# Mixed keys of the HGRN2 layer in two buffers: VectorE writes the updated half into the next level's buffer, GpSimd brings only the resting half

## What is computed

```python
def step(state, inp):                      # per head, forward; the backward pass flips time
    qc, kc, vc, gc = inp
    b = jnp.cumsum(gc, axis=2)             # gc = log f, f the forget gate
    diff = b[:, :, :, None, :] - b[:, :, None, :, :]
    decay = jnp.exp(jnp.where(causal, diff, -jnp.inf))
    attn = jnp.einsum('bhid,bhjd,bhijd->bhij', qc, kc, decay)
...
o_f = _gla_chunks(qh, k_f, vh, lf_f)
o_b = flip(_gla_chunks(flip(qh), flip(k_b), flip(vh), flip(lf_b)))
```

## Time and profile of the kernel before

| | us |
|---|---|
| median of 3 runs | 1420.4 (1419.1 to 1421.58) |
| the profiled execution's own time | 1419.64 |
| its span, first to last instruction | 1417.8 |
| TensorE matmul busy | 1355.3 (96%) |
| VectorE busy | 511.1 (36%) |
| GpSimd busy | 176.6 (12%) |
| heads of the HGRN2 layer | about 690 to 1026 of the span |

### The profile page before, as it was taken

How to read it: one execution, slowest core, us unless ns; L and a number is a source line. 1 busy time by engine, 2 the same in 40 slices (tenths; PEclk the granted TensorE clock), 3 DMA queues, 4 the chain that set the end, 5 groups by cost and what they waited for, 6 DMA issues and landing times.

```text
span 1417.8 us, 16281 instructions
## 1 busy us (share of the span) xinstructions
PE 1355.3 (96%) x6751; PEld 611.1 (43%) x6751; DVE 511.1 (36%) x908; ACT 193.9 (14%) x327; POOL 176.6 (12%) x118
## 2 busy tenths in 40 slices
PE   8999999989999999799999999999799999999995
PEld 4444464633333333344555555555446333333322
DVE  1244863432111111520455556555545221111107
ACT  1025400100000000111111111111011000000000
POOL 0000400050000001100222233222200400000020
PEclk9999989999999999999999999999999999999998
DMA  9920155468999994543222102200094789999952
GB/s 348 356 73 1 73 224 207 175 241 311 416 406 426 409 426 181 214 119 131 60 60 60 40 21 59 59 0 0 1 384 190 276 330 421 410 423 409 388 206 91
DMA packets 82888, 305.75 MB, mean 216 GB/s; under 512 B 5444, under 2 KB 49800, under 8 KB 70408
## 3 DMA queue, kind: packets, MB, share of 16 engines
q1 hardware_dynamic: 61728, 262.81, 47.7%
q10 hardware_dynamic: 16488, 25.21, 4.9%
q0 software_dynamic: 4608, 16.78, 3.1%
HBM read 271.23 MB, written 33.55 MB: 215 GB/s over the span
## 4 chain that ended last, share of the span: by engine, by line
PE 67%; issue 21%; DVE 6%; POOL 3%; ACT 1%; ACTq 1%; DVEq 0%; POOLq 0%
PE ps L559 24%; PE ps L594 11%; PE ps L460 8%; PE ps L517 7%; PE ps L702 4%; POOL W L1586 2%; PE ps L715 2%; PE ps L544 2%; PE ps L509 1%; PE ps L582 1%; PE ps L613 1%; PE ps L485 1%; PE ps L498 1%; PE ps L651 1%; PE ps L524 1%
## 5 line engine op out<-in xcount | busy, mean ns | idle before, releaser
L559 PE MATMUL ps<-W,S 128*32 128x512 f32 (+1 forms) x2048 | 336.7, 597 | 2.3 <-DVE S L1397 2.3
L715 PE MATMUL ps<-hT,W 128*128 128x512 f32 x512 | 232.5, 593 | 0.7 <-ACT W L845 0.7
L559 PE MATMUL ps<-S 128*64 128x512 f32 (+1 forms) x512 | 223.1, 593 | 0.5 <-DVE S L1397 0.5
L594 PE MATMUL ps<-W,hT 128*32 128x512 f32 (+1 forms) x1024 | 171.4, 594 | 1.7 <-DVE hT L1411 1.0
L559 PEld LDWEIGHTS ps<-W,S 128*32 128x32 f32 (+1 forms) x2048 | 97.9, 114 | 148.0 <-issue 143.7
L715 PEld LDWEIGHTS ps<-hT,W 128*128 128x128 f32 x512 | 92.8, 191 | 90.3 <-issue 88.5
L594 PE MATMUL ps<-S,hT 128*32 128x512 f32 (+1 forms) x256 | 113.2, 594 | 1.0 <-issue 1.0
L1586 POOL TENSOR_TENSOR W<-S,sq 128x512 f32<-128x512 f32 x56 | 83.8, 1497 | 145.3 <-DVE S L1494 110.6
L845 ACT ACTIVATE hT<-ps 128x512 f32<-128x512 f32 x82 | 46.5, 599 | 387.4 <-PE ps L594 287.0
L559 PEld LDWEIGHTS ps<-S 128*64 128x64 f32 (+1 forms) x512 | 61.8, 123 | 71.9 <-issue 70.5
L460 PE MATMUL ps<-W,hT 128*128 128x512 f32 x192 | 83.0, 593 | 0.7 <-ACT hT L845 0.7
(11 more groups left out here) (231 smaller groups left out, 1332.3 us busy)
## 6 DMA issues: line engine op xcount, KB each, us to landing
W<-moe_w_gate SPq DMA_DIRECT2D x24, 2048.0 KB, 12.5
W<-moe_w_up SPq DMA_DIRECT2D x24, 2048.0 KB, 13.2
W<-moe_w_down SPq DMA_DIRECT2D x24, 2048.0 KB, 11.4
S<-moe_w_gate SPq DMA_DIRECT2D x8, 2048.0 KB, 13.6
S<-moe_w_up SPq DMA_DIRECT2D x8, 2048.0 KB, 13.4
S<-moe_w_down SPq DMA_DIRECT2D x8, 2048.0 KB, 16.7
W<-w_in_odd SPq DMA_DIRECT2D x32, 512.0 KB, 6.3
slot_rows<-S ACTq DMA_DIRECT2D x4, 2816.0 KB, 19.4
```

The source lines that it names most:

```text
L559: last = pe.matmul(ps[a:a + n, bank, :], xgT[:, c, a:a + n], w[L][slot_of(e)][:, c, :], start=(c == 0), stop=(c == ND - 1))
L594: last = pe.matmul(ps[a:a + n, 2 + half, :], hidT[:, c, a:a + n], wd[L][slot_of(e)][:, c, half * 512:(half + 1) * 512], start=(c == 0), st ...
L715: last = pe.matmul(ps[:, f % 2, :], ring[slot][:, f, c, :], hT[:, c, :], start=(c == 0), stop=(c == ND - 1))
```

## The change

`K2` keeps its meaning for the keys that rest at a level. The mixed keys now live in `km[u % 2]`. VectorE multiplies those that stay mixed at the next level (the outer quarters of each 4s block) straight into `km[(u + 1) % 2]`, and writes the other updated ones (the inner quarters) to `K2`; both are instructions of 256 elements, and both are issued ahead of VectorE's wait for level u's own matmuls. GpSimd brings the 256 resting keys of the next level from `K2` into the other quarters of the buffer, one level earlier than its whole copy came, and runs eight such copies a head. The long-range products read `km`. `prepare` writes the mixed keys of level 1 and the rest by two strided tensor_scalar of 512 elements in place of one of 1024, and `ksum` adds the two under alternating rows.

```diff
@@ -239,7 +239,7 @@
         off_ps, off_done = sem("off_in_psum"), sem("off_done")
         hpv_ps, hout_done, hsq_done, sq_added = (sem(n) for n in (
             "hpv_in_psum", "hout_done", "hsq_done", "sq_added"))
-        keys_updated, keys_mixed = sem("keys_updated"), sem("keys_mixed")
+        keys_updated, keys_joined = sem("keys_updated"), sem("keys_joined")
         ssq_ps, rms_var, rms_std, rms_done = sem("ssq_in_psum"), sem("rms_var"), sem("rms_std"), sem("rms_done")
         stored = sem("out_stored")
         dve_order, pool_order = sem("dve_order"), sem("pool_order")
@@ -723,9 +723,8 @@
                     pe.wait_ge(prepped, hd + 1)
                 if level == 2:
                     pe.wait_ge(diag_done, hd + 1)
-                if level >= 1:
-                    pe.wait_ge(keys_mixed, hd * LEVELS + level)
                 if level >= 2:
+                    pe.wait_ge(keys_joined, hd * 8 + level - 1)
                     pe.wait_ge(updated, hd * 8 + level - 1)
                 if level >= 3:
                     pe.wait_ge(level_done, hd * LEVELS + level - 2)
@@ -740,19 +739,21 @@
 
             def gram_off(hd):
 
+                pe.wait_ge(keys_joined, hd * 8 + 7)
                 pe.wait_ge(updated, hd * 8 + 7)
                 for j in range(NT):
                     i = j ^ 1
-                    last = pe.matmul(ps[:, 4, j * P:(j + 1) * P], K2[:, j % 2, j * P:(j + 1) * P],
+                    last = pe.matmul(ps[:, 4, j * P:(j + 1) * P], km[0][:, j * P:(j + 1) * P],
                                      Q2[:, i % 2, i * P:(i + 1) * P], start=True, stop=True)
                 last.then_inc(off_ps, 1)
 
             def gram_pairs(hd):
+                pe.wait_ge(keys_joined, hd * 8 + 8)
                 pe.wait_ge(updated, hd * 8 + 8)
                 for j in range(NT):
                     i = 1 - j // 2
                     last = pe.matmul(ps[:, 5 + j // 2, (j % 2) * 256:(j % 2 + 1) * 256],
-                                     K2[:, j // 2, j * P:(j + 1) * P],
+                                     km[1][:, j * P:(j + 1) * P],
                                      Q2[:, i, i * 256:(i + 1) * 256], start=True, stop=True)
                 last.then_inc(off_ps, 1)
 
@@ -1453,7 +1454,10 @@
                     dve.wait_ge(off_ps, hd * 2)
                 lb, olb, nw = (a[:, bass.ds(hd, 1)] for a in (col("lb"), col("olb"), prm[:, R_NW:R_NW + HG]))
                 v.tensor_scalar(FF, stg[:, 4:6, :], olb, lb, ALU.mult, ALU.add)
-                v.tensor_scalar(K2, stg[:, 6:8, :], olb, None, ALU.mult)
+                v.tensor_scalar(view(km[1], 0, [[2, T // 2], [1, 2]]), view(stg, 6 * T, [[2, T // 2], [T + 1, 2]]),
+                                olb, None, ALU.mult)
+                v.tensor_scalar(view(K2, T, [[2, T // 2], [1 - T, 2]]), view(stg, 7 * T, [[2, T // 2], [1 - T, 2]]),
+                                olb, None, ALU.mult)
                 v.scalar_tensor_tensor(qs, stg[:, 0, :], float(P) ** -0.5, stg[:, 1, :], ALU.mult, ALU.mult
                                        ).then_inc(prep_in, 1)
                 if not first:
@@ -1463,7 +1467,8 @@
                 v.scalar_tensor_tensor(sg, stg[:, 2, :], nw, stg[:, 3, :], ALU.mult, ALU.mult)
                 dve.wait_ge(prep_in, hd + 1)
                 v.tensor_tensor(Q2, view(qs, 0, [[0, 2], [1, T]]), FF, ALU.mult)
-                v.tensor_tensor(ksum, K2[:, 0, :], K2[:, 1, :], ALU.add).then_inc(prepped, 1)
+                v.tensor_tensor(view(ksum, 0, [[2, T // 2], [1, 2]]), view(km[1], 0, [[2, T // 2], [1, 2]]),
+                                view(K2, T, [[2, T // 2], [1 - T, 2]]), ALU.add).then_inc(prepped, 1)
 
             def segment_products(s):
 
@@ -1486,14 +1491,23 @@
                     v.tensor_tensor(view(to, at2, [[step2, 2], [1, n]]), view(src, at, [[step, 2], [2, n]]),
                                     view(src, at + 1, [[step, 2], [2, n]]), ALU.mult)
 
+                now, after, m = km[u % 2], km[(u + 1) % 2], n // 2
+                if u > 1:
+                    dve.wait_ge(keys_joined, hd * 8 + u - 1)
+                    dve.wait_ge(gram_ps, hd * 8 + u)
+                if u < 8:
+                    v.tensor_tensor(view(K2, T + s, [[4 * s, m], [s - T, 2], [1, s]]),
+                                    view(now, s, [[4 * s, m], [s, 2], [1, s]]),
+                                    view(src, at, [[4, m], [step + 3, 2], [0, s]]), ALU.mult)
+                v.tensor_tensor(view(after, 0, [[4 * s, m], [3 * s, 2], [1, s]]),
+                                view(now, 0, [[4 * s, m], [3 * s, 2], [1, s]]),
+                                view(src, at + step + 1, [[4, m], [1 - step, 2], [0, s]]), ALU.mult
+                                ).then_inc(keys_updated, 1)
                 if u < 8:
                     dve.wait_ge(gram_ps, hd * 8 + u + 1)
                 else:
                     dve.wait_ge(off_ps, hd * 2 + 1)
-                q, k = mixed(Q2, s, 0, T), mixed(K2, s, 0, T)
-                v.tensor_tensor(k, k,
-                                view(src, at + step + 1, [[2, n], [-(step + 1), 2], [0, s]]), ALU.mult
-                                ).then_inc(keys_updated, 1)
+                q = mixed(Q2, s, 0, T)
                 v.tensor_tensor(q, q,
                                 view(src, at + 1, [[2, n], [step - 1, 2], [0, s]]), ALU.mult).then_inc(updated, 1)
 
@@ -1575,17 +1589,17 @@
                 if not first:
                     pool.wait_ge(hpv_ps, hd)
                 pool.tensor_copy(vh, v1[:, :, bass.ds(hd * P, P)]).then_inc(vh_done, 1)
-                for level in range(1, LEVELS + 1):
-                    s = 1 << (level - 1)
-                    if level == 1:
+                for level in range(2, 10):
+                    s = 1 << (level - 2)
+                    if level == 2:
                         pool.wait_ge(prepped, hd + 1)
                     else:
-                        pool.wait_ge(keys_updated, hd * 8 + level - 1)
-                    if level >= 3:
+                        pool.wait_ge(keys_updated, hd * 8 + level - 2)
                         pool.wait_ge(gram_ps, hd * 8 + level - 1)
-                    pool.tensor_tensor(view(km[level % 2], 0, [[2 * s, T // (2 * s)], [s, 2], [1, s]]),
-                                       mixed(K2, s, 0, T), view(ones, 0, [[0, T // (2 * s)], [0, 2], [0, s]]), ALU.mult
-                                       ).then_inc(keys_mixed, 1)
+                    m = T // (4 * s)
+                    pool.tensor_tensor(view(km[level % 2], s, [[4 * s, m], [s, 2], [1, s]]),
+                                       view(K2, s, [[4 * s, m], [T + s, 2], [1, s]]),
+                                       view(ones, 0, [[0, m], [0, 2], [0, s]]), ALU.mult).then_inc(keys_joined, 1)
                 pool.wait_ge(hsq_done, hd + 1)
                 if first:
                     pool.wait_ge(pool_order, 3)
```

## The result

The changed kernel took 1403.44 us (median, 1401.94 to 1405.0), the kernel before 1420.49 beside it: ratio 0.9884 (95% interval 0.9872 to 0.9896), 17.0 us faster. 1411.5 was forecast, 1407 to 1417 as the range: the direction is right, the size is nearly twice what I gave. Two more comparisons, on two chips, gave 0.9910 (0.9896 to 0.9924) and 0.9886 (0.9869 to 0.9902). The changed kernel's medians agree (1403.44, 1403.84, 1403.91); the kernel before beside it moved (1420.49, 1416.94, 1419.24), so the gain was 17.0, 13.1 and 15.3 us. The profiled execution took 1403.62, its span is 1401.7 (before: 1419.64 and 1417.8), 16.1 shorter.

A forecast was written before the change was run, and what follows sets the result against it. TensorE, busy 96% of the span, was taken as the bound, with gains only where it waits for VectorE and GpSimd. Level 2 4.5 + head 7 7.6 - `ksum` 3.2 = 8.9 us, giving 1411.5 us, range 1407 to 1417.

The forecast's parts named there:

- Heads 0 to 5 show the same picture: Heads 0 to 5 were taken to be like head 6: 3.47 us rounds without idle time, only level 2 late.
- The other levels gain 0: In heads 0 to 6, levels other than level 2 were said to gain 0, matmuls and filler filling the round.
- Level 2's own wait: Heads 0 to 6: level 2 no longer waits 0.64 us for GpSimd's copy; gain 4.5 us in seven heads.
- point (b): `ksum` reads one operand by single elements from alternate rows: +0.46 us in seven heads, 3.2 us lost.
- Head 7's round: Head 7 after level 2: VectorE's sequence sets the round, from 3.45 to 2.33 us; five rounds gain 5.6 us.
- the pair in `prepare`: Two strided key instructions replace one: at worst 1.5 us more a head, covered by VectorE's idle 3.04, counted 0.
- (c): First update of a head: key work before the level 1 matmuls ends some 3.0 us after `prepped`, costing nothing.
- 1: Head 7: GpSimd's reads block VectorE's query update, 0.7 us in six rounds, taking 4.2 of the gain: 1415.7; chance 0.18.
- 2: Head 7: VectorE keeps up and the round falls to TensorE's 1.95 us, 2.3 more gain: 1409.2; chance 0.07.
- 3: `ksum` grows by 1.1 us instead of 0.46 in seven heads, 4.5 more lost: 1416.0; chance 0.07.
- 4: All heads: VectorE becomes the bound; at 3.6 us a round 4 us slower, 1424.6; chance 0.06.
- 5: Each level: new waits put GpSimd back in front, the 12.8 us idle stays: 1419 to 1421; chance 0.07.

The follow-up runs named there:

- e1: Kernel before, but GpSimd copies only the first 256 of the 512 mixed keys from level 2 on; ratio 0.9941 to the kernel before.
- e2: Kernel before with TensorE's loop over heads 2 to 5 written out, other engines' loops kept; ratio 0.9974 to the kernel before.
- e5: Changed kernel, but resting keys are also written in full to K2 and ksum adds its two plain rows; ratio 0.9874 to the kernel before.
- e4: Changed kernel with GpSimd's half copies released one level later; ratio 0.9912 to the kernel before.
- e6: Changed kernel, but GpSimd adds the previous head's squares and copies the head's values behind its eight half copies; ratio 0.9858 to the kernel before.
- e7: Changed kernel with the edits of e5 and e6 together, run twice; ratios 0.9846 and 0.9854 to the kernel before.
- e3: Changed kernel with VectorE's wait for the level's own matmuls moved ahead of its two key instructions; ratio 0.9920 to the kernel before.

## Why the prediction came out wrong

- **The step that failed** is "Heads 0 to 5 show the same picture" and, from it, "The other levels gain 0". Heads 2 to 5 had rounds of 3.60, in the chain through GpSimd, with TensorE's loop making the answer slower (e1, e2). From level 2 on they gained 0.77 a head, 3.1 us in four heads, where I gave 0. The other three heads gained 0.08 each at level 2 to 3. Level 2's own wait was right: 4.7 against 4.5.
- **`ksum`**, point (b): the price of three alternating operands was taken for one; 3.2 forecast, 1.0 measured. The estimate in the prediction from the Trainium skill, "Vector Engine (DVE) Microarchitecture Reference", Measured stream behaviour, 0.35 each, was nearer but also more than twice the 0.14 to 0.15 of the rows.
- **Head 7's round**: 2.33 forecast, 2.13 to 2.26 measured. The structure was right (VectorE is the bound, level 1 to 2 takes 2.80 to the digit). I had priced every round by level 3's products and a mean of 0.45 for a half; the products shrink from 0.29 to 0.17, and a half is 0.42. With the last interval 0.8 us more than forecast.
- These are 3.3 + 2.2 + 0.8 and, from level 2's wait, 0.2: the 6.5 us that the heads gained beyond 8.9, 15.4 in all. What is left of the 17.0 of the first comparison lies outside the heads and is not explained; the other two comparisons gave 13.1 and 15.3.
- **Right**: what bounds head 7, that `ksum` moves the start of heads 1 to 7 (e5), that the pair in `prepare` is covered (it takes 1.0, less than the 1.4 to 2.3 named as its sign, and 2.7 of idle time is left before the output), that (c) costs nothing. **Rivals**: 1 is a real mechanism (e4) but does not act in this kernel; 2 half came true, with the round near 2.15 at the high levels, though VectorE remained the bound; 3, 4 and 5 did not happen.

## What to carry to other kernels

Compare the distance between rounds in every head that runs the same code, in a loop or written out, and look at the weight loads' waits beside the matmuls': TensorE's matmul rows abutted here while a chain through GpSimd held it, and 0.13 us a round over 24 rounds is 3 us. Price an access pattern by how many operands have it, and look for pairs of VectorE and GpSimd instructions that are released together in front of a critical step: moving GpSimd's two by half a head was worth as much as a quarter of this whole change. A product that is needed one step later belongs ahead of the wait for this step: here that was nearly half of the gain in the VectorE-bound head.

## What the runs showed of the hardware

**Exclusion.** VectorE's `tensor_tensor` instructions with both inputs in SBUF and GpSimd's instructions, which read SBUF, held each other up here: `Q2` 2.29 beside GpSimd and 1.22 when GpSimd's two are moved (e6, e7), the query update 0.69 or 1.08 by who starts first (e4), the half copy 0.61 when it starts first (e4) and 0.91 to 1.44 beside or behind VectorE. The Trainium skill, "SBUF — State Buffer", Who interferes with whom, states that two such instructions contend for a port pair that only one of them holds at a time, and all these rows agree.

**A wait in TensorE's loop answers later.** From the end of GpSimd's copy to the next weight loads it took 0.21 to 0.25 us in the loop (head 3) and 0.05 to 0.06 in the part that is written out (head 6); with the loop written out (e2) it is 0.05 in head 4. That the cause is the register values in the loop's waits is argued, not shown.

**TensorE's clock.** The stall at head 7's level 0 was the same 2.2 to 2.3 us in ten profiles, but the granted clock behind it was not. First the changed kernel, then e5; the stretch before level 0 and the one from it (its length, then PE busy, ..., PEclk third from the end):

```profile
978.08:982.58 4.50, 1.95 (x4) 0.68 (x4) 4.22 (x5) 0.60 (x1) 2.90 (x2) 1.00 0.00 0
982.58:985.08 2.50, 2.50 (x9) 2.15 (x10) 2.32 (x3) 0.39 (x1) 1.25 (x1) 0.52 0.00 0
```

```profile
977.30:981.80 4.50, 1.96 (x5) 0.68 (x5) 4.22 (x5) 0.60 (x1) 2.90 (x2) 1.00 0.00 0
981.80:984.30 2.50, 2.50 (x14) 2.02 (x15) 2.33 (x3) 0.60 (x1) 1.25 (x1) 1.00 0.00 0
```

0.52 after the one, 1.00 after the other, the work ahead being alike. In seven of the ten (both of before, three of the changed kernel, e2, e4) the granted clock over the first 5 us from level 0 is 0.66 or 0.67, so much of that time at 1.2 GHz, and level 0 to level 2 of head 7 takes 1.4 to 1.7 us longer; in e1, e3 and e5 it is 1.00, all of it at 2.4 GHz. With the stall at 0.7 to 0.8 (e6 and both runs of e7) it is 1.00 in three of three. What decides between the two in the ten is open. It can be part of why medians of one kernel differ (1416.8 to 1421.0 for the kernel before), and of why e5 measured more than its edit is worth.
